# The experts' down matrix and activations split in two fp32r parts, its four pieces in the ring of the gate and up pieces

## The reference, cut to what matters

```
# 32 experts; each token goes to 2 of them; per expert a block of its tokens
xb = h_pad[tok]                                          # rows x 1024
yb = (silu(xb @ w1[e]) * (xb @ w3[e])) @ w2[e]           # w1, w3: 1024 x 512, w2: 512 x 1024
return yb * wt[:, None]
```

## Time and profile before

| what | value |
|---|---|
| time, median of 3 runs (lowest, highest) | 1992.23 us (1987.92, 1994.1) |
| the profiled execution's own time | 1995.2 us |
| its span | 1993.4 us |
| mean granted clock over the span | 0.926 |
| busy over the span: PE, DVE, ACT, POOL | 84%, 57%, 42%, 14% |
| experts: first and last copy of a result | 1318.7 and 1936.7 us from the span's start |
| DMA packets over the span | 355.21 MB |

### The profile page before, as it was taken

One profiled execution on the slowest core, in us unless ns is written; L12 is line 12 of the kernel. 1 busy time (PEld: TensorE's weight loads), 2 busy tenths in 40 slices (PEclk: granted clock), 3 DMA queues, 4 the chain that ended last, 5 costly groups with the idle time before them and its releaser, 6 DMA issues. The chain is left out here.

```text
span 1993.4 us, 41463 instructions
## 1 busy us (share of the span) xinstructions
PE 1670.0 (84%) x17095; PEld 1259.8 (63%) x17095; DVE 1128.4 (57%) x1818; ACT 844.0 (42%) x1325; POOL 288.6 (14%) x371
## 2 busy tenths in 40 slices
PE   5999999958985989889873993099999999999980
PEld 4777777846754777777762773076666666666650
DVE  4568888637654444444348333366565656565636
ACT  5256666302221434434333110066555656565632
POOL 0010000011111333333331000400000000000003
PEclk9999999979997999999895996599999999999995
DMA  5225544341102211111411115369898989998927
GB/s 170 71 85 142 151 118 121 106 159 52 64 22 72 72 56 57 57 56 57 188 56 67 65 63 208 131 262 377 346 378 360 375 348 376 361 378 347 378 115 263
DMA packets 99905, 355.21 MB, mean 178 GB/s; under 512 B 17304, under 2 KB 56519, under 8 KB 85160
## 3 DMA queue, kind: packets, MB, share of 16 engines
q1 hardware_dynamic: 86568, 306.83, 41.3%
q0 software_dynamic: 8576, 29.37, 3.9%
q10 hardware_dynamic: 4608, 16.78, 2.1%
HBM read 294.72 MB, written 56.13 MB: 176 GB/s over the span
## 5 line engine op out<-in xcount | busy, mean ns | idle before, releaser
L2292 DVE TENSOR_TENSOR e_rl<-proj,e_rh 128x1024 fp32r<-128x1024 f32 x256 | 305.0, 1223 | 149.9 <-ACT e_rh L2233 148.7
L2233 ACT ACTIVATE e_rh<-proj 128x1024 fp32r<-128x1024 f32 x256 | 258.6, 1053 | 82.5 <-PEq L1940 50.6
L51 PE MATMUL e_ph<-e_rh,e_xh 128*128 128x512 f32 x512 | 221.5, 433 | 16.9 <-DVE e_rl L2292 14.3
L2219 PE MATMUL e_py<-mix,proj 128*128 128x512 f32 x512 | 225.0, 592 | 0.7 <-issue 0.7
L51 PE MATMUL e_ph<-e_rh,e_xl 128*128 128x512 f32 x512 | 201.8, 394 | 0.0
L51 PE MATMUL e_ph<-e_rl,e_xh 128*128 128x512 f32 x512 | 200.4, 391 | 0.0
L51 PE MATMUL a_b<-a_xh,a_wh 128*128 128x512 f32 x432 | 177.7, 411 | 5.7 <-DVE a_wl L587 3.2
L51 PE MATMUL a_b<-a_xh,a_wl 128*128 128x512 f32 x432 | 169.8, 393 | 0.0
L51 PE MATMUL a_b<-a_xl,a_wh 128*128 128x512 f32 x432 | 169.8, 393 | 0.0
L2219 PEld LDWEIGHTS e_py<-mix,proj 128*128 128x128 f32 x512 | 97.1, 190 | 110.6 <-issue 108.1
L51 PEld LDWEIGHTS e_ph<-e_rh,e_xh 128*128 128x128 f32 x512 | 97.2, 190 | 47.6 <-DVE e_rl L2292 20.7
(11 more groups left out here) (358 smaller groups left out, 3192.7 us busy)
## 6 DMA issues: line engine op xcount, KB each, us to landing
proj<-in_moe_w SPq DMA_DIRECT2D x64, 2048.0 KB, 14.4
mix<-in_moe_w SPq DMA_DIRECT2D x32, 2048.0 KB, 8.6
proj<-scan_operands SPq DMA_DIRECT2D x64, 320.0 KB, 4.1
expert_rows<-e_yo ACTq DMA_DIRECT2D x32, 512.0 KB, 11.1
scan_operands<-late SPq DMA_DIRECT2D x56, 256.0 KB, 2.6
proj<-in_w_in SPq DMA_DIRECT2D x27, 512.0 KB, 4.2
proj<-in_x SPq DMA_DIRECT2D x16, 512.0 KB, 6.2
expert_rows<-proj SPq DMA_DIRECT2D x1, 7680.0 KB, 24.0
```

What stands on the lines that cost most here:

```text
L51: m = e.matmul(out, lhs[a], rhs[b], start=first and n == 0, stop=last and n == 2)
L2219: m = e.matmul(py[h][:, :], at[:, k, :], w2[j][:, k, h * HALF:(h + 1) * HALF], start=(k == 0), stop=(k == KF - 1))
L2233: e.activation(rh[s % RING][:, :], piece(j, s), ACT.Copy).then_inc(high, 1)
L2292: e.tensor_tensor(rl[s % RING][:, :], piece(j, s), rh[s % RING][:, :].bitcast(F32), ALU.subtract).then_inc(low, 1)
```

## The change

- Four pieces are added to the eight: 8 to 11 are the four 128x1024 slices of w2 (`PIECES = 12`), with high and low parts in the same ring. The activations get a high part (`ath`, ScalarE) and a low part (`atl`, VectorE). The down step is four calls of a new `down`, each six fp32r matmuls, in place of the float32 matmuls.
- The ring's order is TensorE's order: 3 to 7, then 0', 1', 2', then 8 to 11 (`STREAM`); without a next expert 3 to 11 (`END`). A piece's tile follows from its place in that order. Three pieces of the next expert (`AHEAD = 3`) are used before the down step instead of two.
- TensorE waits behind piece 11 until its own matmuls are counted in `used`, and then counts `down_done`.
- ScalarE: the next rows and Silu stand between pieces 6 and 7 (before: behind 7); the high activations between 8 and 9; both halves of the result are copied by ScalarE.
- VectorE: the next rows behind piece 7; the product with the gate behind 2' (before: behind 1'); the low activations between pieces 9 and 10 (behind all of them for the last expert).
- SP: the load of the next w2 waits for the low part of piece 11 instead of `down_done`.

In the diff the lines taken out are left out; the listing above has them.

```diff
--- before.py
+++ after.py
@@ -2113,7 +2113,13 @@
         idx = [sb(f"e_idx{j}", [P, 1], U32) for j in range(2)]
         xh, xl = ([sb(f"e_{n}{j}", [P, KD, P], F32R) for j in range(2)] for n in ("xh", "xl"))
...
+        RING, PIECES = 4, 12
+        AHEAD = 3
+        STREAM = list(range(AHEAD, 8)) + [PIECES + s for s in range(AHEAD)] + list(range(8, PIECES))
+        END = list(range(AHEAD, PIECES))
...
+                return w2[j][:, s - 8, :]
             return (w1, w3)[s // 4][j][:, 2 * (s % 4):2 * (s % 4) + 2, :].rearrange("p k f -> p (k f)")
+        def at_ring(s):
+            return s % RING
...
@@ -2152,9 +2164,8 @@
                 with e.Fori(1, NP) as i:
                     for j in range(2):
                         n = i * 2 + (j - 2)
...
+                        for k, count in enumerate((n * PIECES + (AHEAD + 1), n * PIECES + 8, n * PIECES + (AHEAD + PIECES))):
+                            e.wait_ge(low, count)
                             e.sem_inc(passed, 1)
                             load_matrix(e, A, room, k, j, i * 2 + j, w_in[j][k])
...
+                def up(j, at, s):
+                    e.wait_ge(low, at + 1)
+                    r = at_ring(s)
                     for q in range(2):
                         k, cut = 2 * (s % 4) + q, slice(q * HALF, (q + 1) * HALF)
                         m = split_matmul(e, ph[s // 4][:, :], (xh[j][:, k, :], xl[j][:, k, :]),
...
+                                         (rh[r][:, cut], rl[r][:, cut]), k == 0, k == KD - 1)
                     m.then_inc(used, 1)
...
+                def down(at, s, r):
+                    e.wait_ge(low, at + 1)
+                    for h in range(2):
+                        cut = slice(h * HALF, (h + 1) * HALF)
+                        m = split_matmul(e, py[h][:, :], (ath[:, s - 8, :], atl[:, s - 8, :]), (rh[r][:, cut], rl[r][:, cut]),
+                                         s == 8, s == PIECES - 1)
+                    m.then_inc(used, 1)
+                def turn_act(n):
                     e.wait_ge(act_ready, n + 1)
                     for k in range(KF):
                         m = e.transpose(pa[:, k, :], act[:, k:FF:KF], S.ident[:, :])
                     m.then_inc(a_turned, 1)
+                def expert(j, n, half_n, next_half):
+                    at = lambda i: n * PIECES + (AHEAD + i)
+                    for s in range(AHEAD, 8):
+                        up(j, at(s - AHEAD), s)
+                        if s == AHEAD and next_half is not None:
+                            turn(1 - j, next_half)
+                    i = 8 - AHEAD
                     if next_half is not None:
...
+                        e.wait_ge(x_low, n + 2)
+                        e.wait_ge(silu, n + 1)
+                        for s in range(AHEAD):
+                            up(1 - j, at(i + s), s)
+                            if s == 0:
+                                turn_act(n)
+                        i += AHEAD
+                    else:
+                        turn_act(n)
+                    e.wait_ge(a_low, n + 1)
                     e.wait_ge(y_kept, n * 2 + 2)
...
+                    for s in range(8, PIECES):
+                        down(at(i + s - 8), s, (AHEAD + i + s - 8) % RING)
+                    e.wait_ge(used, at(i + PIECES - 8))
+                    e.sem_inc(down_done, 1)
                 turn(0, 0)
                 e.wait_ge(x_low, 1)
...
+                for s in range(AHEAD):
+                    up(0, s, s)
                 run_experts(e, expert)
...
@@ -2239,58 +2265,68 @@
                         m = e.activation(xh[j][:, 4 * q:4 * q + 4, :], tp[q][:, :, :], ACT.Copy)
                     m.then_inc(x_high, 1)
+                def first_pieces(j, at, half_n):
+                    for i, s in enumerate(range(AHEAD, 2 * AHEAD)):
+                        if s == 4:
+                            e.wait_ge(w_in[j][1], half_n * 16 + 16)
+                        if i or at is not None:
+                            e.wait_ge(used, i if at is None else at + i)
+                        split(j, s, s % RING)
                 def expert(j, n, half_n, next_half):
...
+                    order = STREAM if next_half is not None else END
+                    for i, s in enumerate(order):
+                        if i < AHEAD:
+                            continue
+                        if s == PIECES:
+                            e.wait_ge(w_in[1 - j][0], next_half * 16 + 16)
+                        if s == 8:
+                            e.wait_ge(w_in[j][2], half_n * 16 + 16)
+                        e.wait_ge(used, n * PIECES + (AHEAD + i - RING + 1))
+                        if s == 7:
+                            if next_half is not None:
+                                rows(1 - j, n + 1)
+                            e.activation(act, ph[0][:, :], ACT.Silu).then_inc(silu, 1)
+                        if s == 9 and next_half is not None:
+                            keep_act(n)
+                        split(1 - j if s >= PIECES else j, s % PIECES, (AHEAD + i) % RING)
                     if next_half is not None:
...
+                        first_pieces(1 - j, n * PIECES + PIECES, next_half)
+                    else:
+                        keep_act(n)
                     e.wait_ge(down_done, n + 1)
                     e.wait_ge(stored[j], half_n * 16 + 16)
...
+                    for h in range(2):
+                        e.activation(yo[j][:, h * HALF:(h + 1) * HALF], py[h][:, :], ACT.Copy).then_inc(y_kept, 1)
                     e.wait_ge(y_kept, n * 2 + 4)
                     e.sem_inc(passed, 1)
                     e.dma_start(S.ys[ds(n, 1), :, :].rearrange("o p d -> (o p) d"), yo[j][:, :]).then_inc(stored[j], 16)
+                def keep_act(n):
+                    e.wait_ge(a_turned, n + 1)
+                    e.activation(ath[:, :, :], pa[:, :, :], ACT.Copy).then_inc(a_high, 1)
                 e.sem_inc(stored[0], 16)
                 e.sem_inc(stored[1], 16)
                 e.sem_inc(y_kept, 2)
                 e.wait_ge(w_in[0][0], 16)
...
+                for s in range(AHEAD):
+                    split(0, s, s)
                 rows(0, 0)
...
+                first_pieces(0, None, 0)
                 run_experts(e, expert)
                 for j in range(2):
                     e.wait_ge(stored[j], NP * 16 + 16)
             @block.vector
...
@@ -2300,27 +2336,35 @@
                     m.then_inc(x_low, 1)
                 def expert(j, n, half_n, next_half):
...
+                    order = STREAM if next_half is not None else END
+                    for i, s in enumerate(order):
+                        if i < AHEAD:
+                            continue
+                        if s == 8:
+                            e.wait_ge(used, n * PIECES + (AHEAD + 8 - AHEAD))
+                            e.wait_ge(silu, n + 1)
+                            e.tensor_tensor(act, act, ph[1][:, :], ALU.mult).then_inc(act_ready, 1)
+                        if s == 10 and next_half is not None:
+                            keep_act(n)
+                        split(1 - j if s >= PIECES else j, s % PIECES, (AHEAD + i) % RING, n * PIECES + (AHEAD + i))
+                        if s == 7 and next_half is not None:
+                            rows(1 - j, n + 1)
                     if next_half is not None:
...
+                        for i in range(AHEAD):
+                            split(1 - j, AHEAD + i, (AHEAD + i) % RING, n * PIECES + (PIECES + AHEAD + i))
+                    else:
+                        keep_act(n)
+                def keep_act(n):
+                    e.wait_ge(a_high, n + 1)
+                    e.tensor_tensor(atl[:, :, :], pa[:, :, :], ath[:, :, :].bitcast(F32), ALU.subtract).then_inc(a_low, 1)
+                for s in range(AHEAD):
+                    split(0, s, s, s)
                 rows(0, 0)
...
```

More of the change, by code:

```diff
@@ L2132, in piece @@
         def piece(j, s):
+            if s >= 8:
+                return w2[j][:, s - 8, :]
             return (w1, w3)[s // 4][j][:, 2 * (s % 4):2 * (s % 4) + 2, :].rearrange("p k f -> p (k f)")
+        def at_ring(s):
+            return s % RING
         def experts_in_order(body):
@@ L2154, in _ @@
                         n = i * 2 + (j - 2)
-                        for k, (done, count) in enumerate(((low, n * PIECES + RING), (low, n * PIECES + PIECES),
-                                                           (down_done, n + 1))):
-                            e.wait_ge(done, count)
+                        for k, count in enumerate((n * PIECES + (AHEAD + 1), n * PIECES + 8, n * PIECES + (AHEAD + PIECES))):
+                            e.wait_ge(low, count)
                             e.sem_inc(passed, 1)
@@ L2186, in turn @@
                     m.then_inc(turned, 1)
-                def up(j, n, s):
-                    e.wait_ge(low, n * PIECES + (s + 1))
+                def up(j, at, s):
```

(50 more changed lines are left out.)

5 lines of the change are left out of this document (2 added, 3 removed).

## The result

The changed kernel takes 2109.7 us in the median (2103.69 to 2111.53, 4 runs) against 1992.66 (1987.92 to 1994.1, 4 runs) before: ratio 1.0586, 95% interval 1.0558 to 1.0615. It is 5.9% slower; the forecast was 2100.8. The profiled execution has a span of 2109.7 against 1993.4 us, +116.3.

What follows compares the result with a forecast made beforehand. TensorE bounds the kernel before, a closed line through three engines the changed one. Odd experts 45.1, even 61.5, last 2.0: +108.6 us on the profiled 1995.2 gives 2103.8; less 3.0 to the median, 2100.8 us, range 2062 to 2145.

Steps and rivals of the forecast that it cites:

- TensorE's work: Down step: 24 fp32r matmuls take 5.5 us instead of 6.86, gain 1.4 us an expert, net 1.0 after the restart.
- The line: Closed path through ScalarE, VectorE and TensorE between result copies: 22.05 us for odd experts (+2.82), 24.99 for even ones (+4.10).
- the timetable: Foretold times of one odd expert after its first result copy: piece 8 at 16.22, next result copy at 22.05 us.
- SUMS: Rival theory of the experiments: ScalarE's and VectorE's added splitting work sets the spacing, wherever it stands; no chance given.
- What is hidden: TensorE's restart wait, pieces 0' to 2', 10, 11 and 3' to 5' lie beside the path; uncovered, the restart costs 12 us.
- Table loads: Both loads per pair stay, on the path in even experts: 1.53 us before piece 6 and 1.41 before Silu.
- First and last expert: Expert 0 counts as even, +4.10 us; the last, without successor, goes from 17.6 to 19.1 + 0.5, +2.0 us.
- Sum: Whole kernel: 45.1 us for odd experts, 61.5 for even ones, 2.0 for the last; together +108.6 us.
- Rival, the clock: TensorE's clock falls in holes of 2.6 us in even experts, slowing the down step: +36, 2137 us; chance 0.13.
- sign of being wrong: TensorE above 95% busy, result spacing below 20 us, or matmuls at a pitch of 0.43 in mid-stage.
- Rival, TensorE stays the bound: The ring of four keeps VectorE ahead at product and low activations: -32, 1960 us; chance 0.07.
- the number the prediction set: TensorE becomes the bound once 3.8 of the 22.05 us between odd results are gone.

Runs made afterwards that it cites:

- fourth experiment: Changed kernel without TensorE's wait for its own last matmul behind piece 11; ScalarE waits for the count of used pieces directly: 2101.05 us, ratio to before 1.0535.
- experiments 1 and 2: Changed kernel, one edit each: product with the gate behind low part of 0', 2066.62 us; low activations before low part of piece 9, 2069.73 us.
- the last version: Changed kernel with all the order edits, small early Silu, both result halves on ScalarE, 6' split before the result copies, 7' before the store: 1952.3 us, ratio 0.9801.
- seventh experiment: Changed kernel with a one-column Silu ahead of piece 6 in each even expert, so one table load serves: 2089.09 us, ratio to before 1.0474.
- no loads: Changed kernel with Copy in place of Silu, so the loop needs no table loads: 2069.04 us, ratio to before 1.0375.
- sixth experiment: Kernel before with its down step's 8 float32 matmuls replaced by 24 fp32r ones on ready tiles, no splits or new order: 1947.58 us, ratio 0.9769.

## Why the prediction was right, point by point

- *TensorE's work*: foretold -1.4 us an expert by itself, measured alone -44.5/31 = -1.44 (the stage holds 31 experts).
- *The line*: spacing 22.05 and 24.99 foretold, 22.23 and 25.08 measured (means of 16 and 14, by 1346.66, 1371.74, 1393.98 and their like; from result 0 to result 30 it is 706.7 us against my 702.7). The 4 us between them lie at the end of the line: piece 8 starts 0.14 later than in the timetable and the next result copy 0.19. Piece 8 comes 0.23 behind the end of the low activations (1671.26 + 0.68 to 1672.17), where I had 0.06. The count's detour over TensorE's queue takes part as well: without it an odd step is 0.21 shorter (fourth experiment). Two shifts of one instruction each (experiments 1 and 2) gave back 40 and 38 us without taking work away, as a line can and sums can't; by SUMS both should have done nothing, and the last version has the splits of the changed kernel and TensorE at 98%.
- *What is hidden*: the restart behind TensorE's own wait is, as said; taking the wait away brought 5 us in thirty experts, not 12. What it is worth where TensorE is the bound, as in the last version, was not measured.
- *Table loads*: both stay and stand on the line, 2.5 us a pair by measurement; the term was 0.2 too large for the loads and 0.1 too small for the loop's return, which I had put together.
- *First and last expert*: result 0 came at 1324.4 instead of 1318.7, +5.7. Of this 1.7 is already there at the first rows' transposes, ahead of the change; 4.0 against 4.1 foretold. The last expert was mis-sized: 21.7 us instead of 19.1. TensorE stood idle 4.39 us ahead of piece 8, and the matmuls behind it show the lower of the two clock levels (changed kernel, TensorE):

```profile
2044.18 0.80 PE L51 MATMUL e_py<-e_rh,e_ath 128*128 128x512 f32 x1 [4.39 <-DVE e_atl L2361]
...
2045.19 0.63 PE L51 MATMUL e_py<-e_rh,e_atl 128*128 128x512 f32 x1
2045.62 0.63 PE L51 MATMUL e_py<-e_rh,e_ath 128*128 128x512 f32 x1
...
2052.35 0.39 PE L51 MATMUL e_py<-e_rh,e_atl 128*128 128x512 f32 x1
```

  They have a pitch of 0.43 instead of 0.23 for the first 13 of 24: 13 x 0.2 = 2.6 us, the whole miss. In the seventh experiment only 6 are that slow behind the same idle time, and the last expert takes 20.2 us, 1.5 less. The sum had the idle time but put the clock behind it at nothing.
- *Sum*: 1.7 (ahead of the change) + 4.0 + (706.7 - 600.5) + (21.7 + 0.5 - 17.6) = 116.5 against a span that grew by 116.3. My 108.6 missed the 1.7, 4 on the line and 2.6 in the last expert.
- *Rival, the clock*: it did fall in mid-stage, which the prediction had named as a sign of being wrong. All of the experts 2, 4, ... 28 have a hole of 2.2 us ahead of piece 7; behind it 7 of these 14 show 6 to 11 matmuls at the lower level. Expert 4 has the longest such spell, and the granted clock from 1404 to 1412 us is 0.57 (changed kernel, TensorE):

```profile
1401.01 0.39 PE L51 MATMUL e_ph<-e_rh,e_xl 128*128 128x512 f32 x1
1403.56 0.50 PE L51 MATMUL e_ph<-e_rh,e_xh 128*128 128x512 f32 x1 [2.16 <-DVE e_rl L2329]
...
1405.89 0.80 PE L51 MATMUL e_ph<-e_rh,e_xh 128*128 128x512 f32 x1 [0.68 <-DVE e_rl L2329]
1406.48 0.63 PE L51 MATMUL e_ph<-e_rl,e_xh 128*128 128x512 f32 x1
...
1411.39 0.63 PE L51 MATMUL e_ph<-e_rl,e_xh 128*128 128x512 f32 x1
```

  It cost next to nothing, since it fell where TensorE has time to spare and not on the down step, as the rival had it: expert 4 takes 25.43 us, the other six 25.04 to 25.08, the seven without a spell 25.03 to 25.09. So the forecast held, though its sign of being wrong came true; the sign should have named the place. In the two runs on the changed kernel whose longest mid-stage idle of TensorE is 1.2 us (no loads, one load) no matmul of mid-stage is at the lower level.
- *Rival, TensorE stays the bound*: it did not. It becomes the bound again once the line is shorter: odd experts reach 18.42 us with both halves on ScalarE, when product, low activations and rows have moved and TensorE's own wait is out, and go no lower when copies and store leave the line as well. That 22.2 - 18.4 = 3.8 is the number the prediction set is in part luck, since its 18.2 held the restart's 0.4, which is gone here; TensorE's own work is nearer the 17.8 of the sixth experiment, and the 0.6 between them are stops that were not taken apart.

## What to carry to other kernels

When work is added to engines that have time to spare, don't compare sums only: write down one round of the loop as a timetable in each engine's program order and look for a closed path through all engines; its length is the period. An instruction that others wait for belongs as early in its engine's order as its operands allow, in front of work that is merely prefetched; here such moves, with every split kept, one table load less in a pair and TensorE's own wait taken out, turned 5.9% slower into 2.0% faster; the one table load less is worth 0.9% in the kernel before by itself. In a loop that mixes simple functions with one from a table, call the one from the table first.

## What the runs showed of the hardware that was not expected

- Behind the same idle time of 2.2 us TensorE's clock fell in 7 of 14 even experts, for 6 to 11 matmuls, and held in the other 7 (granted 0.98 over 550 us). Behind one of 4.39 us it was lower for 13 matmuls in the changed kernel and for 6 in the seventh experiment. Where TensorE has time to spare such a spell doesn't show in the kernel's time.
- A wait of 1 us on TensorE costs 1.25 us from start to start, with the wait's tail and a first step of 0.33 instead of 0.23.
- Stages that no edit touched shift by up to 9.1 us between profiles of like kernels, more than the smallest effects looked for; the time from first to last result copy tells these apart, the median doesn't.
